# Attention in a hybrid decoder layer: P normalised before it is turned, P times V in two fp32r parts, and more taps in the GLU stage

## The reference, cut to what matters

```python
hn = rms_norm(h_res, gain); part = lambda i: hn @ w_in[:, o[i]:o[i+1]]
q, k, v, fg, glu_in, gate_a, gate_c = ...
# attention: cum = cumsum(log_sigmoid(fg + b_forget)), causal, query blocks of 128
s = einsum('bqhd,bkhd->bhqk', q, k) * HEAD_DIM ** -0.5 + cum[q] - cum[k]
p = softmax(where(causal, s, -inf))
a = einsum('bhqk,bkhd->bqhd', p, v) @ w_attn_out
# convolution module
u = glu_in[..., :D] * sigmoid(glu_in[..., D:])
c = silu(layer_norm(sum_j w[j] * u[t - 30 + j] + b)) @ w_conv_out + b_conv_out
h = h_res + (sigmoid(gate_a) * a + sigmoid(gate_c) * c) @ w_out
y = rms_norm(h + square(relu(rms_norm(h) @ w_up)) @ w_down)[:, 16:]
```

## Time and profile before

| | before |
|---|---|
| median of 3 runs | 977.45 us (976.29 to 978.54) |
| profiled execution, its own time | 977.84 us |
| its span, first to last instruction | 976.0 us |
| mean granted TensorE clock | 0.997 |
| PE, DVE, ACT, POOL busy | 955.8, 601.6, 406.3, 30.2 us |

### The profile page before, as it was taken

One profiled execution on the slowest core, in us unless ns is written; L12 is line 12 of the kernel. 1 busy time (PEld: TensorE's weight loads), 2 busy tenths in 40 slices (PEclk: granted clock), 3 DMA queues, 4 the chain that ended last, 5 costly groups with the idle time before them and its releaser, 6 DMA issues.

```text
span 976.0 us, 14595 instructions
## 1 busy us (share of the span) xinstructions
PE 955.8 (98%) x5342; PEld 820.6 (84%) x5342; DVE 601.6 (62%) x920; ACT 406.3 (42%) x701; POOL 30.2 (3%) x45
## 2 busy tenths in 40 slices
PE   5999999999999999999999999999999999999997
PEld 4999998888888888887788888788888888888886
DVE  6566678788787887875775665543344334434433
ACT  6422345455454554544683244432143224223322
POOL 2000010000000000001200000000000000000000
PEclk9999999999999999999999999999999999999999
DMA  8333332121212121222232532233333223332322
GB/s 224 88 87 96 96 86 68 47 66 44 65 43 65 45 63 44 65 66 65 70 103 87 191 90 87 86 106 91 106 87 108 87 86 107 90 104 87 90 82 87
DMA packets 153433, 84.27 MB, mean 86 GB/s; under 512 B 3023, under 2 KB 151503, under 8 KB 153392
## 3 DMA queue, kind: packets, MB, share of 16 engines
q1 hardware_dynamic: 152768, 83.37, 29.5%
q0 software_dynamic: 592, 0.29, 0.2%
q10 hardware_dynamic: 32, 0.07, 0.1%
HBM read 81.55 MB, written 2.16 MB: 86 GB/s over the span
## 4 chain that ended last, share of the span: by engine, by line
PE 95%; DVE 3%; DMA 1%; ACT 1%; issue 0%; SPq 0%; DVEq 0%
PE pj L991 61%; PE pj L987 19%; PE pTO L1094 5%; PE pTO L1092 2%; PE pTO L1080 2%; PE pS L1068 1%; PE pS L1067 1%; DVE cv L854 1%; PE pj L1236 1%; DMA ga<-in_x_dram 1%; PE pTO L1078 1%; PE pj L1015 1%; DVE ga L962 1%; PE pTO L1149 0%; PE pTO L1138 0%; DVE in_lo L706 0%
## 5 line engine op out<-in xcount | busy, mean ns | idle before, releaser
L451 ACT ACTIVATE w_hi<-raw 128x1024 fp32r<-128x1024 f32 x145 | 152.4, 1051 | 161.5 <-PE pj L991 131.1
L991 PE MATMUL pj<-in_hi,w_hi 128*128 128x512 f32 x512 | 205.5, 401 | 0.5 <-DVE w_lo L687 0.5
L991 PE MATMUL pj<-in_lo,w_hi 128*128 128x512 f32 x512 | 205.6, 402 | 0.0
L687 DVE TENSOR_TENSOR w_lo<-raw,w_hi 128x1024 fp32r<-128x1024 f32 x145 | 178.6, 1231 | 42.4 <-ACT w_hi L451 42.4
L991 PE MATMUL pj<-in_hi,w_lo 128*128 128x512 f32 x512 | 201.5, 394 | 0.0
L744 DVE SCALAR_TENSOR_TENSOR cv<-u,prm,cv 128x512 f32<-128x512 f32 (+1 forms) x240 | 181.6, 759 | 9.5 <-DVE cv L744 5.8
L991 PE MATMUL pj<-mid_hi,w_hi 128*128 128x512 f32 x368 | 144.4, 392 | 0.0
L991 PE MATMUL pj<-mid_hi,w_lo 128*128 128x512 f32 x368 | 143.3, 389 | 0.0
L991 PE MATMUL pj<-mid_lo,w_hi 128*128 128x512 f32 x368 | 143.2, 389 | 0.0
L991 PEld LDWEIGHTS pj<-in_hi,w_hi 128*128 128x128 f32 x512 | 96.4, 188 | 22.7 <-DVE w_lo L687 1.0
L991 PEld LDWEIGHTS pj<-in_hi,w_lo 128*128 128x128 f32 x512 | 96.5, 188 | 18.8
(11 more groups left out here) (186 smaller groups left out, 984.3 us busy)
## 6 DMA issues: line engine op xcount, KB each, us to landing
raw<-in_w_in_dram SPq DMA_DIRECT2D x57, 512.0 KB, 3.8
raw<-in_w_mlp_up_dram SPq DMA_DIRECT2D x32, 512.0 KB, 4.0
raw<-in_w_mlp_down_dram SPq DMA_DIRECT2D x32, 512.0 KB, 3.7
raw<-in_w_attn_out_dram SPq DMA_DIRECT2D x8, 512.0 KB, 3.7
raw<-in_w_conv_out_dram SPq DMA_DIRECT2D x8, 512.0 KB, 3.7
raw<-in_w_out_dram SPq DMA_DIRECT2D x8, 512.0 KB, 3.7
ga<-in_x_dram SPq DMA_DIRECT2D x4, 512.0 KB, 7.3
cv<-in_x_dram SPq DMA_DIRECT2D x1, 2048.0 KB, 8.7
```

The costliest lines, as they stand in the source:

```text
L451: A(w_hi[:, c % SPLIT, :], raw[:, c % RAW, :], ACT.Copy).then_inc(s_hi, 1)
L687: V.tensor_tensor(w_lo[:, c % SPLIT, :], raw[:, c % RAW, :], w_hi[:, c % SPLIT, :].bitcast(F32), ALU.subtract).then_inc(s_lo, 1)
L991: last = mm(prod(c), wt, src[:, at:at + NT], **flags)
```

## The change

P is normalised before it is turned. DVE finds the minimum (`row_least`), ACT the exponential (`exponential`), DVE the reciprocal in the same step (`sum_reciprocal(s)`), ACT multiplies the block by it in a further pass (`normalise`, one step later). The block lies in `prob` so that it can be turned in q+2 whole key tiles of 128, of which the last is padded with zeros (`pads`, set once after the decay rows have been written, and waited for by PE through `s_pads` before the first pair). It is turned at the end of the step, behind product 11 (`CUTS`). One step later again ACT copies the turned P to `pt_hi` (fp32r, `probs_high`) and DVE subtracts it for `pt_lo` (`probs_low`).

V of a pair is turned one pair later, at step 2 (`values_transpose`, five tiles), and kept for each head as 64 high and 64 low columns beside each other (`v_hl`). P times V (`half_out`) then has v_hl, 128 columns, as the stationary operand and pt_hi and pt_lo of two query blocks as the moving one, 256 wide where both blocks have the key tile. The result is features by tokens, its two halves of 64 partitions are added (`out_copy`, `out_add`), and no turning of the output is left. There are 4 such groups a pair, at steps 3, 5, 7 and 1 of the next.

DVE's order in a step becomes: probs_low(s-2), half of the step's taps, row_least(s), low parts of q, k or V, low(c+1), one tap, the reciprocal of unit s, the other taps. Eleven taps of each tile are in the GLU stage, two are in the steps of k = 0, and 18 are left for the pairs. In k = 9 low(c+1) comes first. Buffers are placed anew, and two small memsets of POOL move.

```diff
-TAPS_EARLY = 7
-TAPS_MID = 1
+TAPS_EARLY = 11
+TAPS_MID = 2
 TAPS_LATE = TAPS - TAPS_EARLY - TAPS_MID
-TAPS_STEP = (3, 3, 3, 3, 3, 3, 2, 3)
-MID_STEP = (0, 0, 2, 2, 0, 0, 2, 2)
+TAPS_STEP = (2, 4, 1, 2, 1, 4, 0, 4)
+MID_STEP = (0, 0, 3, 3, 1, 3, 3, 3)
...
+        def probs(q, first=0, last=None):
+            end = LONG_AT if q % 2 == 0 else LONG_AT + VT
+            at = end - (q + 2) * P
+            return prob[:, at + first:end if last is None else at + last]
+        def turned(q):
+            at = 1024 - (P if q == QT - 1 else 0)
+            return pQ[:, at:at + (q + 2) * P]
+        def cells(buf, q):
+            return buf[:, FIRST_CELL[q] * P:(FIRST_CELL[q] + q + 2) * P]
...
+            at = (512, 0, 512, AT)[q]
...
+            A(dec_rows[0], f_m, ACT.Copy).then_inc(s_f, 1)
+            def exponential(s, k, it=None):
                 U = 8 * k + s
                 wait(act, s_max, U + 1, it, 16)
                 nk = META + P * (s % QT + 1)
...
+                A(probs(s % QT, 0, nk), probs(s % QT, 0, nk), ACT.Exp, bias=nmax[:, s:s + 1], scale=-1.0,
                   accum_out=rsum[:, s:s + 1]).then_inc(s_exp, 1)
...
+            def normalise(s, k, it=None):
                 U = 8 * k + s
+                wait(act, s_rinv, U + 1, it, 16)
+                nk = META + P * (s % QT + 1)
+                A(probs(s % QT, 0, nk), probs(s % QT, 0, nk), ACT.Copy, scale=rinv[:, s:s + 1]).then_inc(s_pn, 1)
+            def probs_high(s, k, it=None):
+                U = 8 * k + s
+                h, q = divmod(s, QT)
                 wait(act, s_T, U + 1, it, 16)
...
+                wait(act, s_pv, 4 * k + 2 * h + q // 2, it, 8)
+                A(cells(pt_hi, q), turned(q), ACT.Copy).then_inc(s_pth, 1)
...
+            def out_copy(h, k, it=None):
+                wait(act, s_pv, 4 * k + 2 * h + 2, it, 8)
+                if h == 0:
+                    wait(act, s_olo, k, it, 2)
+                A(o_sb[h * HD:(h + 1) * HD, :], pO7[HD:P, :], ACT.Copy).then_inc(s_oa, 1)
             def out_high(k, it=None):
...
+                wait(act, s_ob, 2 * k + 2, it, 4)
+                A(feat(mid_hi, count(k, it, 2)), o_sb[:, :], ACT.Copy).then_inc(s_ohi, 1)
...
             def pair_step(s, k, it=None):
                 c = N_PAIR + 4 * k + s // 2
+                attention_head(s, k, it)
                 if s % 2 == 0 and c > N_PAIR:
                     wait(act, s_mm, c, it, 8)
                 if s == 0 and k > 0:
                     A(feat(ga, count(k - 1, it, 2)), prod(c - 1), ACT.Copy).then_inc(s_gev, 1)
...
+                if s == 3:
                     if k == 0:
                         act.wait_ge(s_u, KT + 1)
...
+                    wait(act, s_vl, k, it, 2)
+                    A(vT[:, 0:T], prod(c - 1, T), ACT.Copy).then_inc(s_vev, 1)
                 if s in (4, 6):
                     dst, width, scale, done = (q_a, NT, -HD ** -0.5, s_qh) if s == 4 else (k_a, T, 1.0, s_kh)
                     for h in range(2):
                         A(dst[0:HD, k % 2, h, :], prod(c - 1, width)[h * HD:(h + 1) * HD, :], ACT.Copy,
                           scale=scale).then_inc(done, 1)
...
+                attention_tail(s, k, it)
                 if s == 4:
                     wait(act, s_qh, 2 * k + 2, it, 4)
                     A(q_b[0:HD, k % 2, :, :], q_a[0:HD, k % 2, :, :].bitcast(F32), ACT.Copy).then_inc(s_dup, 1)
...
                     A(k_a[HD:P, k % 2, :, :], k_a[0:HD, k % 2, :, :].bitcast(F32), ACT.Copy).then_inc(s_dup, 1)
                 if s % 2 == 0 and c > N_PAIR:
                     high(c + 1, it, 8)
...
+            def attention_head(s, k, it=None):
                 if s == 0 and k >= 2:
...
+                    normalise(7, k - 2, it)
                 if s > 0 and 1 <= k <= PAIRS:
...
+                    normalise(s - 1, k - 1, it)
+                if s < 2 and k >= 2:
+                    probs_high(s + 6, k - 2, it)
+                if s >= 2 and 1 <= k <= PAIRS:
+                    probs_high(s - 2, k - 1, it)
+                if s == 2 and k >= 2:
+                    out_copy(1, k - 2, it)
+                if s == 3 and k >= 2:
+                    out_high(k - 2, it)
+                if s == 6 and 1 <= k <= PAIRS:
+                    out_copy(0, k - 1, it)
+            def attention_tail(s, k, it=None):
+                if s == 2 and 1 <= k <= PAIRS:
+                    wait(act, s_vT, k, it, 2)
+                    wait(act, s_pv, 4 * (k - 1), it, 8)
+                    A(v_hl[:, :, :, 0:HD], pV.rearrange("p (t h d) -> p t h d", h=2, d=HD), ACT.Copy).then_inc(s_vh, 1)
                 if 1 <= k <= PAIRS:
...
+                    exponential(s, k - 1, it)
...
+            dve.wait_ge(s_decw, 32)
+            for cell in (3, 8):
+                V.memset(pads[:, cell, META:P], 0.0).then_inc(s_pads, 1)
+            def row_least(s, k):
                 U = 8 * k + s
                 nk = META + P * (s % QT + 1)
...
+                wait(dve, s_S, U + 1)
+                wait(dve, s_T, U - 1)
+                V.tensor_tensor_reduce(probs(s % QT, 0, nk), scores(s % QT), mask[:, T - nk:T], 1.0, 3.0e38,
                                        ALU.add, ALU.min, nmax[:, s:s + 1]).then_inc(s_max, 1)
...
+            def sum_reciprocal(s, k):
                 U = 8 * k + s
...
+                wait(dve, s_exp, U + 1)
                 V.reciprocal(rinv[:, s:s + 1], rsum[:, s:s + 1]).then_inc(s_rinv, 1)
...
+            def probs_low(s, k):
+                q = s % QT
+                wait(dve, s_pth, 8 * k + s + 1)
+                V.tensor_tensor(cells(pt_lo, q), turned(q), cells(pt_hi, q).bitcast(F32),
+                                ALU.subtract).then_inc(s_ptl, 1)
+            def out_add(h, k):
+                wait(dve, s_oa, 2 * k + h + 1)
+                o = o_sb[h * HD:(h + 1) * HD, :]
+                V.tensor_tensor(o, pO7[0:HD, :], o, ALU.add).then_inc(s_ob, 1)
+            def out_low(k):
+                wait(dve, s_ohi, k + 1)
+                V.tensor_tensor(feat(mid_lo, k), o_sb[:, :], feat(mid_hi, k).bitcast(F32),
+                                ALU.subtract).then_inc(s_olo, 1)
+            def taps(s, k, first, last):
                 for i in range(sum(TAPS_STEP[:s]) + first, sum(TAPS_STEP[:s]) + last):
...
+                    tap(TAPS_EARLY + TAPS_MID + i, k - 1, KT * (TAPS_EARLY + TAPS_MID) + TAPS_LATE * (k - 1) + i)
+            def attention_head(s, k):
+                if s < 2 and k >= 2:
+                    probs_low(s + 6, k - 2)
+                if s >= 2 and 1 <= k <= PAIRS:
+                    probs_low(s - 2, k - 1)
+                if s == 2 and k >= 2:
+                    out_add(1, k - 2)
+                if s == 6 and 1 <= k <= PAIRS:
+                    out_add(0, k - 1)
+                if s == 3 and k >= 2:
+                    out_low(k - 2)
+            def pair_step(s, k):
+                c = N_PAIR + 4 * k + s // 2
+                attention_head(s, k)
+                early = TAPS_STEP[s] // 2
                 if 1 <= k <= PAIRS:
...
+                    taps(s, k, 0, early)
+                    row_least(s, k - 1)
                 if s in (4, 6) and k < PAIRS:
...
                     hi, dst, rows, width, scale, ready, done = (
                         (q_a, q_a, slice(HD, P), NT, -HD ** -0.5, s_qh, s_ql) if s == 4 else
                         (k_a, k_b, slice(0, HD), T, 1.0, s_kh, s_kl))
                     for h in range(2):
...
+                        wait(dve, ready, 2 * k + 2)
+                        V.scalar_tensor_tensor(out=dst[rows, k % 2, h, :],
+                                               in0=prod(c - 1, width)[h * HD:(h + 1) * HD, :], scalar=scale,
+                                               in1=hi[0:HD, k % 2, h, :].bitcast(F32), op0=ALU.mult,
                                                op1=ALU.subtract).then_inc(done, 1)
...
+                if s == 2 and 1 <= k <= PAIRS:
+                    wait(dve, s_vh, k)
+                    V.tensor_tensor(v_hl[:, :, :, HD:P], pV.rearrange("p (t h d) -> p t h d", h=2, d=HD),
+                                    v_hl[:, :, :, 0:HD].bitcast(F32), ALU.subtract).then_inc(s_vl, 1)
+                if s % 2 == 0 and c > N_PAIR:
+                    low(c + 1)
                 if k == 0:
                     for i in range(sum(MID_STEP[:s]), sum(MID_STEP[:s + 1])):
                         j, m = divmod(i, KT)
                         tap(TAPS_EARLY + j, m, KT * (TAPS_EARLY + j) if j == 0 else KT * TAPS_EARLY + i - KT + 1)
...
                 if 1 <= k <= PAIRS:
...
+                    if early < TAPS_STEP[s]:
+                        taps(s, k, early, early + 1)
+                    sum_reciprocal(s, k - 1)
+                    taps(s, k, early + 1, TAPS_STEP[s])
+            for k in range(PAIRS + 1):
                 for s in range(8):
                     pair_step(s, k)
...
+            for s in range(8):
+                if s % 2 == 0:
```

(74 more changed lines are left out.)

277 lines of the change are left out of this document (90 added, 187 removed).

## The result

The changed kernel takes 1076.74 us (median of 4 runs, 1076.5 to 1078.13), the kernel before 977.03 beside it on the same chip: ratio 1.102, 95% interval 1.100 to 1.104, so 10% slower. The forecast was 1053 us, in a range of 1008 to 1085. The profiled execution's span went from 976.0 to 1074.7 us, +98.7.

What follows compares the result with a forecast made beforehand. PE was taken to bound the kernel before, at 38.4 us a pair. Ring 48.6, GLU 8.4, pads 15.7, clock 1.5 and end 1.5 made +75.7 us on 977.84: 1053 us, range 1008 to 1085.

Steps and rivals of the forecast that it cites:

- The ring: In the pairs, DVE and ACT take turns waiting for each other: 45.2 us a pair against 38.4, +48.6 us.
- the 10% rival: In the pairs, DVE and ACT overlap, PE's 32.9 us stays the bound: 959 us, chance 10%.
- The favoured case: In the pairs, DVE and ACT waiting in turn with PE at full clock: 1053 us, 1033 to 1072, chance 53%.
- the rival of 25%: In the pairs, PE's clock also halves behind waits, 2.4 us a pair, +19: 1072 us, chance 25%.
- Pads: Ahead of the first pair's V chunk, PE waits for DVE's memsets behind the decay transfers: +15.7 us.
- GLU: In the GLU stage, four more taps make DVE the bound, 12.9 us a tile instead of 11.75: +8.4 us.
- The clock at the restart: After the wait for the pads, PE restarts with 3 us at half clock: +1.5 us.
- The end of the pairs: Behind the last pair, low(c+1) ahead of probs_low costs about 2.5 us, less four output transposes: +1.5 us.
- What I had put at nothing: After the pairs, buffer places and in_hi's stride change no instruction count: no effect on time.

Runs made afterwards that it cites:

- Two cuts: Two runs against the changed kernel: DVE's tap and reciprocal ahead of the low parts, 1006.29 us; ACT's high(c+1) ahead of the exponential, 1020.16 us.
- The placed kernel: Changed kernel with stages a step apart and pads first, plus P times V at step end and output and V work on DVE and ACT later: 956.17 us.
- the filled kernel: Changed kernel with 18 or 26 overwritten PE products ahead of all four waits for pt_lo in a pair: 1065.27 us.

## Why the prediction was right, and where it was off

*The ring: right in kind.* Two cuts, each of which changes only an order, take 7 to 9 us from a pair, and with all stages a step apart the same arithmetic takes 34.8 instead of 48.1. The low busy sum of DVE (31.0 of 32.9 us) had to be set aside for this, and rightly: PE's busy time fell and the span grew. The case of the 10% rival, PE as the bound at 959 us, did not come with this order. The placed kernel comes near to it in kind, with PE busy 194.8 of 200 us; that its time, 956, is so near is chance, since the 959 count the wait for the pads, 12 us that this kernel has not, and a pair of 32.9 us where it takes 34.8.

*The favoured case: missed.* The ring at full clock, 53%, had a range of its own, 1033 to 1072, and 1077 lies above it. What came is nearest to the rival of 25%, ring and falling clock together, at 1072.

*The term that was mis-sized* is the ring's period, 45.2 against 48.0 us a pair (48.1 less the 0.07 of the yardstick): 7 x 2.8 = 20 of the 23 us between 75.7 and 98.7. Most of it is the clock, which the sum put at nothing in the pairs and which I had as a rival with 25% ("The clock falls in the waits"), arguing against it that PE is busy most of the time. That did not keep it up. PE is busy 196.0 of the 250 us from 200 on, and behind 16 of the 30 waits for pt_lo of 1.5 us or more the clock went to 0.50 for about 3 us: behind all ten of 2.54 us and more, behind six of the 17 from 2.36 to 2.50, behind none of the three of 1.5; with P times V later, also behind one of 1.85. The Trainium skill ("TensorE: Matmul & The Clock Gate", Part 1) has the clock halved after idling; the trace agrees: all 17 falls from 184 to 560 us begin in a wait of more than 2.3 us or within 2 us behind it. The half clock comes into the ring through the transposes, which then end late for ACT:

```profile
ACT pt_hi L563 <- PE pQ L1156: 12.9, 14, 3.3
```

An estimate of the split: each step at its length with the clock at 1.00 (6.21, 4.33, 7.33, 4.85, 6.56, 4.34, 7.28, 4.98 us for s = 0 to 7; steps 1, 2 and 6 from the pairs where they ran short, step 5 from the filled kernel) makes 45.9 us. The pairs between the first and the last took 47.8, so some 2 us a pair are the clock, a little less than the 2.4 that the rival had, and 0.6 are links that I had too short. Most of these lie in step 6 (6.8 forecast), where out_add, the exponential, the doubling of k and the normalise are each about 0.13 over; in the other steps the links are right within about 0.1 us. The first of the seven periods, 49.3 us, holds the rest. Some 4 us more lie in the first and the last pair and were not placed.

*Pads.* 15.7 us worked out, 15.6 measured; the run without that wait gave back 12, because the low parts that DVE issues around its 11 taps come next: in that run PE waits 0.89 us at 127.70 and, after the first V products, 2.86 at 142.27 for w_lo (16.3 - 0.9 - 2.9 = 12.5).

*GLU.* Forecast 12.9 us a tile, and the starts of u at 51.76 and 64.62 in the trace of after give 12.86. With +12 us for the taps alone (8.4 in my sum, the rest between the GLU stage and the end of pair 0) this term was right within its stage and a little small over the program.

*The clock at the restart.* I had 1.5 us. The chain has the V chunk's 48 products at 8.65 us instead of 48 x 0.1225 = 5.88: 2.8.

*The end of the pairs.* From the last scores (443.4 before, 543.2 after) to the next stage's first product (475.6 and 579.0) it grew by 3.6 us, where I had 1.5.

*What I had put at nothing* and was not: the new stride of in_hi after the pairs, -4.7 us (below). Without it the miss would have been 28 us.

## What to carry to other kernels

Where two queues that were seen to go in order feed each other, write down for each instruction what it waits for on the other queue and what stands behind it; if the arrows close within one step, the period is the sum of the links, and no busy share shows it. The cure is to let each stage of a unit be issued a step after the one it needs, before anything is made cheaper: here the same arithmetic took 1077 us in one order and 956 in another (12 of it the pads), where the arithmetic of before took 977. Then move each remaining consumer behind work that waits for nothing, and price PE's waits with the clock that they cost.
